# Two norms of a fused two-block model, taken token piece by token piece across the stage boundary

## The chip, the cores and the metric

The kernel runs on one core of one Trainium2 chip. The metric is device time in microseconds (us) from launch to the last result, median of three runs. All arithmetic is in fp32; most matrix products are split in three products of two reduced-precision parts (below).

## The reference, cut to what matters

Two blocks run one after the other on 1024 tokens of width 1024. Block 1 is one hybrid layer; block 2 puts 16 meta tokens in front and runs two layers.

```
# block 1
x = x + mix @ w_out                      # 8 output units of 128 channels
h2 = rmsnorm(x, norm2_g)                 # mean over the 1024 channels, per token
ff = square(relu(h2 @ w_up)); x = x + ff @ w_down      # d_ff 4096
x = rmsnorm(x, final_g)
# block 2, l = 0, 1
h = rmsnorm_2(h_res, norm_gain[l]); proj = h @ w_in[l]
... pooling, latent attention with rotary angles cos/sin(pos * inv_freq) ...
h_res = h_res + merged @ w_out[l]
```

Each norm needs the squares of all 1024 channels of a token before it can scale any of them, and nothing from other tokens.

## The kernel before

**Layout.** Channels lie on the 128 partitions, in 8 chunks (KC = 8), tokens on the free axis: 1024 columns in block 1, 1044 (16 meta, 1024, 4 padding) in block 2. X is the residual, `Ah`/`Al` (act_hi, act_lo) hold an activation as a rounded high part and a low part, `Wh`/`Wl` (w_hi, w_lo) two slots of weights in the same form. R is a work area of 19 rows. The PSUM tile `acc` has two sides s = 0, 1 with three banks each, `aux` has two banks.

**A unit** is 128 output channels of one matrix: 8 chunks k, for each the products Wh·Ah, Wh·Al, Wl·Ah over all columns, in pieces of 512 columns in block 1 (`PIECES1` = 2 x 512) and 348 in block 2 (`PIECES2` = 3 x 348). So a unit is 48 or 72 matmuls on TensorE (PE). Units alternate the side of `acc` and the weight slot.

**Weights.** SyncE loads each unit's raw weights. GpSimd (POOL) splits them: one cast to Wh (L374), then four subtractions of 256 columns for Wl (L353). It may start on unit n once unit n-2 is done, since the slot must be free. `wide` (L425 inside `matrix`) begins with the products of Wh and waits for Wl later; `wide_two` runs two units side by side, chunk by chunk as the activation arrives, and needs both parts of both units at once.

**The end of a stage.** VectorE (DVE) adds each finished unit to X (L1634), ScalarE (ACT) squares it (L944), DVE adds the square to a total (L1426). After the eighth unit `norm_sum` sums the total over partitions with a matmul of ones (L502). ACT turns that into the scale by Ln and Exp (L949, L952). Then `normalise` on DVE goes through the 8 chunks at full width: multiply (L1433), cast to Ah (L1416), subtract to Al (L1417). PE consumes chunk k as soon as its low part is there.

This happens at two places that the change touches. **Boundary A** lies between block 1's output projection and its feed-forward stage; there the first feed-forward unit runs alone with the arriving chunks (`wide(..., (a_ready, 16))`), and the table of rotary angles (fetch of the positions, 14 DVE operations L1648 to L1665, two sines on ACT L1125 and L1128) follows the norm. The relu that clears `acc` for the third unit (L1138) stands behind the sines in ACT's order. **Boundary B** lies between the first and the second layer of block 2; there `wide_two` runs the first two units side by side. At B, ACT also starts a store of all of X to memory (`spill_x`, L1166), and DVE's pooling (from L1713), which overwrites parts of X, waits for it.

The order on each engine is the order in which the code is written; semaphores join the engines.

Of the kernel before, what the change touches and what calls it, by code (L numbers as in the profile page):

```python
# [7 lines left out]
F32 = mybir.dt.float32  # L8
F32R = mybir.dt.float32r
I32 = mybir.dt.int32  # L10
ALU = mybir.AluOpType
# [125 lines left out]
def build(nc, xT, metaT, pos, params, consts, bands, lru_w, wstream, outT):  # L137
    with ExitStack() as ctx:
# [143 lines left out]
        for name in tuple(f"x_in{j}" for j in range(KC)) + tuple(f"reload{j}" for j in range(KC)) + (  # L282
# [15 lines left out]
            "s_ready", "p_in",  # L298
            "pv_done", "pv_ready0", "pv_ready1", "inv_ready", "inv_used", "av_free0", "av_free1",
# [5 lines left out]
        SQL = ((R[:, 6, :], R[:, 3, :], R[:, 2, :]), (R[:, 7, :], R[:, 1, :], R[:, 0, :]))  # L305

# [94 lines left out]
        def _(pe):  # L401
# [92 lines left out]

            def norm_sum(s, pieces, squares):
# [112 lines left out]
            for j in range(2, KC):  # L608
                wide(j % 2, (j + 1) % 2, PIECES1)
            norm_sum(1, PIECES1, R[:, 8, :])  # L610

            with pe.Fori(0, GROUPS) as i:
                loop = Loop(i, GROUPS, [(unit, FG + 4), (unit_hi, FG + 4), (free[0], FG // 2 + 4),
                                        (free[1], FG // 2 + 4), (c["f_ready"], FG)])
                for j in range(FG):
                    wide(j % 2, (j + 1) % 2, PIECES1, (sems["a_ready"], 16) if j == 0 else None)
                for j in range(4):
                    next_unit()
                    ws = (j + 1) % 2
                    for s in range(2):  # L620
                        if j == 0 and s == 0:
# [3 lines left out]
                               None if s == 0 else sems["unit_done"])  # L625
                loop.end()
            norm_sum(0, PIECES1, R[:, 8, :])

            a_count = 24
            ws0 = N_UNITS1 % 2  # L630
            for l in range(LAYERS):
# [6 lines left out]
                norm_sum(0, PIECES2, R[:, 8, :])  # L638
                wide_two(PIECES2, (sems["a_ready"], a_count), (ws(), ws()))
                for j in range(2, 8):  # L640
                    wide(j % 2, ws(), PIECES2)
                a_count += 8
# [254 lines left out]
                for j in range(2, KC):  # L897
                    wide(j % 2, ws(), PIECES2)
                a_count += 8
# [4 lines left out]
        def _(act):  # L904
# [49 lines left out]
            def norm_stats(src, n, width, pieces, s, slots, rs, dim, eps, arrive):  # L954
# [3 lines left out]
                norm_scale(width, pieces, s, rs, dim, n)  # L958

# [151 lines left out]
            def updated(s):  # L1111
# [5 lines left out]
            norm_stats(lambda j: X[:, j, META:T2], KC, T1, PIECES1, 1, SQ, R[:, 10, :],  # L1117
                       DM, 1e-6, lambda j: updated(j % 2))
            act.dma_start(X[:, :, 0:META], metaT.rearrange("(c p) t -> p c t", p=P)).then_inc(sems["meta_in"], 16)
            act.wait_ge(sems["a_ready"], 24)  # L1120
            act.dma_start(R[:, 8, META:T2].bitcast(I32), pos).then_inc(sems["pos_in"], 16)

            c["to_act"].step()
            act.wait_ge(sems["to_act"], c["to_act"].value())
            do(nc.scalar.activation(R[:, 16, 0:TP], R[:, 16, 0:TP], ACT.Sin))  # L1125
# [256 lines left out]
        def _(dve):  # L1382
# [254 lines left out]
            for j in range(KC):  # L1637
                await_unit()
                add_to_residual(j, j % 2, PIECES1, META, T1)
                if j:  # L1640
                    add_square(j - 1, KC, SQ, full)
# [461 lines left out]
```

## Time and profile before

| | us |
|---|---|
| median of 3 runs (3355.52 to 3359.7) | 3358.72 |
| the profiled execution: its own time | 3356.4 |
| its span, first to last instruction | 3354.6 |
| PE busy in the span | 3057.1 (91%) |
| DVE busy | 1440.9 (43%) |
| POOL busy | 1074.3 (32%) |
| ACT busy | 694.5 (21%) |

The profiled execution's own time is its span and 1.8 us around it; it lies 2.3 us below the median. PE is busy for most of the span, so what counts is where PE stands idle and what ended its wait. Matmul records overlap: the distance of two starts is the cost of one.

### The profile page before, as it was taken

The page shows a single profiled execution, that of the slowest core. Times are in us where ns is not written, and L with a number is a line of the kernel's source. Part 1 is how long each engine was busy: PE and PEld are TensorE (multiplying, and loading weights), DVE is VectorE, ACT ScalarE, POOL GpSimd, SP SyncE. Part 2 cuts the span into 40 slices and gives each one's busy share as a digit, 9 for nine tenths or more (in the row PEclk, how much of TensorE's full clock was granted, in tenths as well). Part 3 has the DMA queues.
Part 4 walks back from the last instruction along what each step waited for, and adds up shares of the span by engine and source line. Part 5 has one row for each costly group of instructions (what it writes and reads, how often), then busy time and mean ns, then how long its engine had stood idle before and what let it go on. Part 6 is the DMA issues. An engine that isn't in the chain of part 4 may idle for free.

```text
span 3354.6 us, 41151 instructions
## 1 busy us (share of the span) xinstructions
PE 3057.1 (91%) x16352; PEld 2688.7 (80%) x16352; DVE 1440.9 (43%) x1730; ACT 694.5 (21%) x1239; POOL 1074.3 (32%) x1335
## 2 busy tenths in 40 slices
PE   6976678899999997799999899989899999999999
PEld 4754556677788775699999788889899999788889
DVE  4678454422222223830011666671820111766661
ACT  2132320000000001100111455510100110455500
POOL 3523013344444443333333211133433432211132
PEclk9988789999999998899999999999899999999999
DMA  2101011111111111211212000051211212000042
GB/s 104 44 32 35 1 63 39 49 46 44 50 44 47 47 44 44 77 51 45 102 45 83 32 14 14 14 185 45 89 51 45 96 51 77 32 16 18 15 178 76
DMA packets 46429, 182.50 MB, mean 54 GB/s; under 512 B 5968, under 2 KB 6096, under 8 KB 45776
## 3 DMA queue, kind: packets, MB, share of 16 engines
q1 hardware_dynamic: 31248, 113.19, 10.6%
q10 hardware_dynamic: 15040, 67.28, 5.3%
q8 instruction: 107, 1.75, 0.2%
q14 instruction: 34, 0.28, 0.0%
HBM read 150.06 MB, written 30.39 MB: 54 GB/s over the span
## 4 chain that ended last, share of the span: by engine, by line
PE 80%; DVE 13%; ACT 3%; issue 2%; POOL 1%; DMA 0%; DVEq 0%; ACTq 0%; POOLq 0%; SPq 0%
PE acc L425 59%; PE aux L824 4%; PE acc L708 4%; PE acc L803 3%; DVE act_lo L1417 2%; PE acc L757 2%; PE acc L692 1%; DVE residual L1482 1%; DVE work L1433 1%; DVE work L1426 1%; PE acc L778 1%; DVE act_hi L1416 1%; PE acc L720 1%; POOL w_lo L353 1%; DVE residual L1505 1%
## 5 line engine op out<-in xcount | busy, mean ns | idle before, releaser
L425 PE MATMUL acc<-act_hi,w_hi 128*128 128x348 f32 (+1 forms) x3104 | 770.6, 349 | 100.7 <-DVE act_lo L1417 41.2
L353 POOL TENSOR_TENSOR w_lo<-w_raw,w_hi 128x256 fp32r<-128x256 f32 (+1 forms) x924 | 817.3, 916 | 17.2
L425 PE MATMUL acc<-act_lo,w_hi 128*128 128x348 f32 (+1 forms) x3104 | 763.9, 346 | 0.0
L425 PEld LDWEIGHTS acc<-act_hi,w_hi 128*128 128x128 f32 x3104 | 546.3, 191 | 162.4 <-issue 68.1
L425 PE MATMUL acc<-act_hi,w_lo 128*128 128x348 f32 (+1 forms) x3104 | 618.8, 345 | 0.0
L425 PEld LDWEIGHTS acc<-act_lo,w_hi 128*128 128x128 f32 x3104 | 548.8, 190 | 43.1
L425 PEld LDWEIGHTS acc<-act_hi,w_lo 128*128 128x128 f32 x3104 | 530.0, 189 | 42.1
L373 POOL TENSOR_TENSOR small<-shape_consts 128x1 f32<-128x1 f32 x192 | 40.9, 213 | 1607.0 <-PE acc L425 1607.0
L425 PE MATMUL acc<-ff_split,w_hi 128*128 128x512 f32 (+1 forms) x1408 | 317.7, 375 | 11.9 <-DVE ff_split L1417 11.9
L1634 DVE TENSOR_TENSOR residual<-acc,residual 128x1024 f32<-128x1024 f32 (+1 forms) x88 | 108.1, 1228 | 473.0 <-PE acc L425 472.9
L425 PEld LDWEIGHTS acc<-ff_split,w_hi 128*128 128x128 f32 x1408 | 253.0, 188 | 60.8 <-DVE ff_split L1417 16.5
L362 POOL CAST w_hi<-w_raw 128x1024 fp32r<-128x1024 f32 x23 | 25.8, 1122 | 632.6 <-PE acc L708 544.4
L1846 DVE TENSOR_REDUCE small<-acc 128x1 f32<-128x512 f32 (+4 forms) x240 | 132.1, 550 | 192.5 <-PE acc L761 121.9
L803 PE MATMUL acc<-ff_split 128*128 128x276 f32 (+5 forms) x864 | 208.4, 354 | 0.0
L374 POOL CAST w_hi<-w_raw 128x1024 fp32r<-128x1024 f32 x192 | 202.5, 1055 | 0.0
L824 PE MATMUL aux<-work 128*128 128x276 f32 (+5 forms) x576 | 177.3, 404 | 0.0
L425 PE MATMUL acc<-ff_split,w_lo 128*128 128x512 f32 (+1 forms) x704 | 166.8, 374 | 0.0
L803 PEld LDWEIGHTS acc<-ff_split 128*128 128x128 f32 x864 | 140.8, 190 | 31.3 <-ACT work L1307 0.5
L1138 ACT ACTIVATE work<-acc 128x1024 f32<-128x1024 f32 x32 | 32.7, 1027 | 627.0 <-PE acc L425 626.4
L932 ACT ACTIVATE work<-acc 64x384 f32<-64x384 f32 (+5 forms) x153 | 93.5, 620 | 289.2 <-PE acc L425 255.7
L1307 ACT ACTIVATE work<-acc 128x384 f32<-128x384 f32 (+2 forms) x240 | 104.2, 435 | 233.9 <-PE acc L803 160.6
L425 PEld LDWEIGHTS acc<-ff_split,w_lo 128*128 128x128 f32 x704 | 127.2, 188 | 22.5
(228 smaller groups left out, 3307.6 us busy)
## 6 DMA issues: line engine op xcount, KB each, us to landing
w_raw<-in_wstream SPq DMA_DIRECT2D x215, 512.0 KB, 3.5
spill_x<-residual ACTq DMA_DIRECT2D x2, 4176.0 KB, 12.2
spill_m<-residual ACTq DMA_DIRECT2D x2, 4176.0 KB, 12.6
spill_g<-work ACTq DMA_DIRECT2D x16, 522.0 KB, 2.7
residual<-spill_m ACTq DMA_DIRECT2D x16, 522.0 KB, 6.1
work<-spill_g ACTq DMA_DIRECT2D x16, 522.0 KB, 8.6
residual<-spill_x ACTq DMA_DIRECT2D x16, 522.0 KB, 4.3
residual<-in_xT ACTq DMA_DIRECT2D x8, 512.0 KB, 9.9
```

Source lines behind the costliest of these rows:

```text
L353: ins = nc.gpsimd.tensor_tensor(Wl[:, s, c0:c0 + w], Wraw[:, s, c0:c0 + w], Wh[:, s, c0:c0 + w].bitcast(F32), ALU.subtract)
L374: nc.gpsimd.tensor_copy(Wh[:, s, :], Wraw[:, s, :]).then_inc(sems["w_hi_done"], 1)
L425: ins = nc.tensor.matmul(acc[0:m, s, p, 0:w], wt[:, ws, w0 + j * m:w0 + j * m + m], x[:, k, p * w:p * w + w], start=(first and t == 0), st ...
L708: ins = nc.tensor.matmul(acc_q[:, 0:w], wt[:, w_head[0], j * P:j * P + P], x[:, j, c0:c0 + w], start=(j == 0 and t == 0), stop=(j == 5 and ...
L757: ins = nc.tensor.matmul(acc_r[bank][:, 0:n], qh[:, min(P * i, LASTQ):min(P * i, LASTQ) + P], kh[:, 512 * p:512 * p + n], start=True, stop ...
L803: ins = nc.tensor.matmul(out, k2[kt][:, c0:c0 + P], q2[qt][:, lo:lo + w], start=m == 0, stop=(m == 2 and not diag))
L824: ins = nc.tensor.matmul(aux[:, b % 2, lo - QP * pc:lo - QP * pc + w], values(h)[:, t, :], prob(k)[:, at:at + w], start=t == 0, stop=end)
L932: return nc.scalar.activation(out, in_, ACT.Copy, scale=scale)
L1307: do(nc.scalar.activation(prob(k)[:, 0:w], src, ACT.Exp), "p_in")
L1417: do(vec.tensor_tensor(lo, src, hi.bitcast(F32), ALU.subtract), name)
L1634: do(vec.tensor_tensor(x, acc_view(s, pieces), x, ALU.add), f"free{s}")
L1846: do(vec.tensor_reduce(S_[:, col:col + 1], acc_r[rough_bank(i, p)][:, 0:n], AX, ALU.max, negate=True), "rough_max")
```

## The change

The last two output units of a stage now run piece by piece: piece 0 of both, then piece 1 of both, and so on (`close_two`). DVE adds a finished piece to X, ACT squares it, and a small matmul into `aux` (`sum_piece`) sums it while PE is in the next piece. DVE and ACT then normalise this piece (`norm_pieces`), ACT making the high part. The first two units of the next stage also run piece by piece (`open_two`); in its first piece the first unit goes four chunks ahead of the second. The order of the steps is the table `NORM_ORDER`. The same is done at A (2 x 512) and at B (3 x 348). The rotary table is computed during the output units before A. `spill_x` at B is issued after the last piece is normalised. The first of the eight feed-forward groups stands outside the loop.

```diff
+        NORM_ORDER = {
+            2: (("add", 0), ("norm", 0, 0, 4), ("add", 1), ("norm", 0, 4, 6), ("norm", 0, 6, 8), ("norm", 1, 0, 8)),
...
+        NORM_SCALE_AFTER = {2: (0, 3), 3: (0, 3, 6)}
+            def sum_piece(p, w):
+                c["piece_total"].step()
+                pe.wait_ge(sems["piece_total"], c["piece_total"].value())
...
+                nc.tensor.matmul(aux[:, p % 2, 0:w], ones, R[:, 8, p * w:p * w + w], start=True,
+                                 stop=True).then_inc(sems["piece_summed"], 1)
+            def close_two(ws, pieces):
+                n, w = pieces
+                for p in range(n):
+                    for s in range(2):
+                        if p == 0:
+                            next_unit()
+                            await_low()
+                            take(s)
+                        for k in range(KC):
+                            ins = piece_products(s, ws[s], p, w, k, k == 0, k == KC - 1)
...
+                            if p and s == 0 and k == 4:
+                                sum_piece(p - 1, w)
+            def open_two(ws, pieces):
...
+                for p in range(n):
+                    ahead = 4 if p == 0 else 0
+                    at = 0
+                    for j in range(KC + ahead):
+                        for s, k in ((0, j), (1, j - ahead)):
...
+                            if k == 0:
+                                if p == 0:
+                                    next_unit()
+                                    await_low()
...
+                            if s == 0:
+                                pe.wait_ge(sems["piece_lo"], lo0 + KC * p + k + 1)
+                            ins = piece_products(s, ws[s], p, w, k, k == 0, k == KC - 1)
...
+                            if p == 0 and at == 8:
+                                sum_piece(n - 1, w)
@@ tensor, boundary A
-            for j in range(2, KC):
+            for j in range(2, KC - 2):
                 wide(j % 2, (j + 1) % 2, PIECES1)
-            norm_sum(1, PIECES1, R[:, 8, :])
...
+            close_two((1, 0), PIECES1)
+            open_two((1, 0), PIECES1)
@@ scalar
+            def norm_pieces(x0, pieces):
...
+                for at, step in enumerate(NORM_ORDER[n]):
...
+                    if step[0] == "add":
...
+                            do(nc.scalar.activation(sq[s][:, cols], X[:, KC - 2 + s, x0 + p * w:x0 + p * w + w],
+                                                    ACT.Square), "piece_squared")
+                    else:
+                        for j in range(step[2], step[3]):
...
+                            do(copy(Ah[:, j, cols], y[j % 2][:, cols]), "piece_hi")
+                    if at in NORM_SCALE_AFTER[n]:
...
+                        act.wait_ge(sems["piece_summed"], c["piece_summed"].value())
+                        do(nc.scalar.activation(R[:, 10, cols], aux[:, p % 2, 0:w], ACT.Ln, scale=1.0 / DM,
+                                                bias=eps_col(1e-6, P)))
+                        after()
+                        do(nc.scalar.activation(R[:, 10, cols], R[:, 10, cols], ACT.Exp, scale=-0.5), "piece_scale")
...
+            act.dma_start(R[:, 13, META:T2].bitcast(I32), pos).then_inc(sems["pos_in"], 16)
+            for j in range(KC - 2):
+                updated(j % 2)
+                square(X[:, j, META:T2], j, [t[:, 0:T1] for t in SQ])
+                if j == 4:
...
+                    do(nc.scalar.activation(R[:, 16, 0:TP], R[:, 16, 0:TP], ACT.Sin))
@@ vector
+            def norm_pieces(x0, pieces, gain):
...
+                            do(vec.tensor_tensor(x, acc[:, s, p, 0:w], x, ALU.add),
+                               "piece_free" if p < n - 1 else f"free{s}")
...
+                    def low(j):
...
+                        do(vec.tensor_tensor(Al[:, j, cols], y[j % 2][:, cols], Ah[:, j, cols].bitcast(F32),
+                                             ALU.subtract), "piece_lo")
...
+                        do(vec.scalar_tensor_tensor(y[j % 2][:, cols], X[:, j, x0 + p * w:x0 + p * w + w],
+                                                    param(gain, j), R[:, 10, cols], ALU.mult, ALU.mult), "piece_y")
+                        if j > step[2]:
+                            low(j - 1)
```

On DVE at boundary A this stood after the totals (STT multiplies, CAST makes the high part, the last row subtracts; one chunk of eight is shown, then the start of the rotary table):

```order
L1433 SCALAR_TENSOR_TENSOR work<-residual,params,work 128x1024
L1416 CAST act_hi<-work 128x1024
L1417 TENSOR_TENSOR act_lo<-work,act_hi 128x1024
L1648 TENSOR_SCALAR work<-work 128x1024
L1649 COPY work<-shape_consts 128x16
L1650 MEMSET work 128x4
L1653 TENSOR_SCALAR work<-work,params 128x1044
```

And now, from the residual adds of piece 0 of the last two units (first row) to the same adds of piece 1 and the first chunks behind them:

```order
L1564 TENSOR_TENSOR residual<-acc,residual 128x512 x2
L1569 TENSOR_TENSOR work<-work 128x512 x2
L1583 SCALAR_TENSOR_TENSOR work<-residual,params,work 128x512 x2
L1576 TENSOR_TENSOR act_lo<-work,act_hi 128x512
L1583 SCALAR_TENSOR_TENSOR work<-residual,params,work 128x512
L1576 TENSOR_TENSOR act_lo<-work,act_hi 128x512
L1583 SCALAR_TENSOR_TENSOR work<-residual,params,work 128x512
L1576 TENSOR_TENSOR act_lo<-work,act_hi 128x512 x2
L1564 TENSOR_TENSOR residual<-acc,residual 128x512 x2
L1569 TENSOR_TENSOR work<-work 128x512 x2
L1583 SCALAR_TENSOR_TENSOR work<-residual,params,work 128x512 x2
```

The casts have left DVE, the operations are half as wide, and four chunks of piece 0 stand ahead of the adds of piece 1.

On ACT at boundary A stood the squares of the eight units, then the scale, two transfers and the sines:

```order
L944 ACTIVATE work<-residual 128x1024 x8
L949 ACTIVATE work<-acc,small 128x1024
L952 ACTIVATE work<-work 128x1024
L1119 DMA residual<-in_metaT 128x8x16
L1121 DMA work<-in_pos 128x1024
L1125 ACT_TABLE_LOAD
L1125 ACTIVATE work<-work 128x1044
```

And now (L1064 squares a piece, L1076 and L1079 are Ln and Exp of a piece's sum, L1018 makes high parts):

```order
L1030 ACTIVATE work<-residual 128x1024
L1064 ACTIVATE work<-residual 128x512 x2
L1076 ACTIVATE work<-aux,small 128x512
L1079 ACTIVATE work<-work 128x512
L1018 ACTIVATE act_hi<-work 128x512 x4
L1064 ACTIVATE work<-residual 128x512 x2
L1018 ACTIVATE act_hi<-work 128x512 x2
L1076 ACTIVATE work<-aux,small 128x512
L1079 ACTIVATE work<-work 128x512
L1018 ACTIVATE act_hi<-work 128x512 x10
```

The scale of piece 1 stands between the high parts of chunks 5 and 6 of piece 0; the sines are no longer behind the scale.

## Rows read from the trace of the kernel before

**Rows 1.** The page: chain that ended last, shares of the span.
```profile
PE 80%; DVE 13%; ACT 3%; issue 2%; POOL 1%; DMA 0%; DVEq 0%; ACTq 0%; POOLq 0%; SPq 0%
```

**Rows 2.** Timeline, PE, boundary A: start, us, engine, line, operation [idle before <-releaser].
```profile
545.56 0.62 PE L425 MATMUL acc<-act_hi,w_hi 128*128 128x512 f32 x2
...
561.79 3.75 PE L502 MATMUL acc<-work,shape_consts 128*128 128x512 f32 x4 [4.95 <-DVE work L1426]
...
571.31 1.19 PE L425 MATMUL acc<-act_hi,w_hi 128*128 128x512 f32 x2 [5.77 <-DVE act_lo L1417]
...
595.87 0.62 PE L425 MATMUL acc<-act_hi,w_hi 128*128 128x512 f32 x2
...
616.14 1.22 PE L425 MATMUL acc<-act_hi,w_hi 128*128 128x512 f32 x2 [8.98 <-ACT work L1138]
...
629.32 0.62 PE L425 MATMUL acc<-act_hi,w_hi 128*128 128x512 f32 x2
...
640.44 1.09 PE L425 MATMUL acc<-ff_split,w_hi 128*128 128x512 f32 x4
```

**Rows 3.** The chain of waits, boundary A: fetch of the positions, first sine.
```profile
594.35 3.44 DMA work<-in_pos
...
612.22 1.08 ACT work L1125
```

**Rows 4.** Timeline, PE, boundary B.
```profile
2328.17 0.64 PE L425 MATMUL acc<-act_hi,w_hi 128*128 128x348 f32 x3
...
2339.62 0.64 PE L425 MATMUL acc<-act_hi,w_hi 128*128 128x348 f32 x3
...
2392.40 0.74 PE L425 MATMUL acc<-act_hi,w_hi 128*128 128x348 f32 x3
...
2403.96 0.64 PE L425 MATMUL acc<-act_hi,w_hi 128*128 128x348 f32 x3
```

**Rows 5.** Groups by line and form, DVE and ACT: xcount | busy us, mean ns | idle before.
```profile
L1822 DVE SCALAR_TENSOR_TENSOR residual<-residual,params 128x384 f32<-128x384 f32 x32 | 19.8, 619 | 1.1
L1599 DVE TENSOR_TENSOR residual<-shape_consts,small 128x512 f32<-128x512 f32 x12 | 8.3, 693 | 0.4
L1826 DVE TENSOR_TENSOR ff_split<-residual,ff_split 128x276 fp32r<-128x276 f32 x16 | 7.1, 447 | 0.6
L1278 ACT ACTIVATE residual<-residual 128x384 f32<-128x384 f32 x32 | 16.8, 524 | 1.0
```

**Rows 6.** Timeline, POOL: the split of one unit's weights, DVE idle, DVE partly and wholly busy.
```profile
489.76 2.83 POOL L353 TENSOR_TENSOR w_lo<-w_raw,w_hi 128x256 fp32r<-128x256 f32 x4
...
2341.18 3.90 POOL L353 TENSOR_TENSOR w_lo<-w_raw,w_hi 128x256 fp32r<-128x256 f32 x4
...
2398.86 6.74 POOL L353 TENSOR_TENSOR w_lo<-w_raw,w_hi 128x256 fp32r<-128x256 f32 x4
```

**Rows 7.** Timeline, DVE, beside the last of these splits, and the end of the pooling.
```profile
2392.24 1.26 DVE L1713 TENSOR_TENSOR residual<-work 128x1059 f32<-128x1059 f32 x1 [2.77 <-ACT work L932]
...
2401.63 1.68 DVE L1713 TENSOR_TENSOR residual<-residual 128x1057 f32<-128x1057 f32 x1
...
2429.96 1.25 DVE L1728 TENSOR_TENSOR work<-acc,work 128x1044 f32<-128x1044 f32 x1
```

**Rows 8.** Timeline, PE: the start behind a wait for weights that POOL had to split.
```profile
1839.44 1.21 PE L425 MATMUL acc<-act_hi,w_hi 128*128 128x348 f32 x3 [4.34 <-POOL w_lo L353]
...
1842.18 0.76 PE L425 MATMUL acc<-act_hi,w_hi 128*128 128x348 f32 x3
```

**Rows 9.** Busy us by engine, then granted clock, DMA share, GB/s, in that stretch.
```profile
1839.00:1842.00 3.00, 2.56 (x9) 2.59 (x10) 0.00 (x0) 0.00 (x0) 0.19 (x1) 0.50 0.48 154
```

**Rows 10.** Timeline, PE: matmuls of 384 columns, each with other operands than the last.
```profile
1998.45 0.34 PE L708 MATMUL acc<-act_lo,w_hi 128*128 128x384 f32 x1
1998.63 0.34 PE L708 MATMUL acc<-act_hi,w_lo 128*128 128x384 f32 x1
```

**Rows 11.** The page: DMA issues, us to landing.
```profile
spill_x<-residual ACTq DMA_DIRECT2D x2, 4176.0 KB, 12.2
```

More of the change, by code:

```diff
@@ new lines, in piece_products @@
+            def piece_products(s, ws, p, w, k, first, end):
+                for t, (wt, x) in enumerate(((Wh, Ah), (Wh, Al), (Wl, Ah))):
+                    ins = nc.tensor.matmul(acc[:, s, p, 0:w], wt[:, ws, k * P:k * P + P],
+                                           x[:, k, p * w:p * w + w], start=(first and t == 0), stop=(end and t == 2))
+                return ins
+            def close_two(ws, pieces):
[8 more added lines that the diff above has]
+                            ins = piece_products(s, ws[s], p, w, k, k == 0, k == KC - 1)
+                            if k == KC - 1:
+                                ins.then_inc(sems["piece_done" if p < n - 1 else "unit_done"], 1)
+                            if p and s == 0 and k == 4:
+                                sum_piece(p - 1, w)
@@ L607, in _, with expand_group @@
             wide_two(PIECES1, (sems["a_ready"], 8), (1, 0))
-            for j in range(2, KC):
+            for j in range(2, KC - 2):
                 wide(j % 2, (j + 1) % 2, PIECES1)
-            norm_sum(1, PIECES1, R[:, 8, :])
[L612 to L616, printed above, removed]
+            close_two((1, 0), PIECES1)
+            open_two((1, 0), PIECES1)
+            def expand_group(first):
+                for j in range(2 if first else 0, FG):
+                    wide(j % 2, (j + 1) % 2, PIECES1)
                 for j in range(4):
@@ L896, in _ @@
                 wide_two(PIECES2, (sems["a_ready"], a_count), (ws(), ws()))
-                for j in range(2, KC):
+                for j in range(2, KC - 2):
                     wide(j % 2, ws(), PIECES2)
+                if l == LAYERS - 1:
+                    for j in range(KC - 2, KC):
+                        wide(j % 2, ws(), PIECES2)
+                else:
+                    close_two((ws(), ws()), PIECES2)
                 a_count += 8
@@ L1421, in add_square @@
+            def add_square(j, n, slots, cols, last="sum_ready"):
                 c["sq_ready"].step()
@@ L1940, in _ @@
                     split(y, Ah[:, j, :], Al[:, j, :], "a_ready")
-                for j in range(KC):
+                for j in range(KC if last else KC - 2):
                     await_unit()
@@ L1945, in _ @@
                     if not last and j:
-                        add_square(j - 1, KC, SQ, wide)
+                        add_square(j - 1, KC - 2, SQ, wide)
                 if not last:
-                    add_square(KC - 1, KC, SQ, wide)
+                    add_square(KC - 3, KC - 2, SQ, wide, "dve_step")
+                    for j in range(KC - 2, KC):
+                        dve.wait_ge(sems[f"reload{j}"], 48 * (l + 1))
 def weight_stream(w):
```

185 lines of the change are left out of this document (136 added, 49 removed).

## The prediction, written before the changed kernel was run

> **What bounds the kernel now.** I read the chain that ended last first: PE holds 80% of it, DVE 13% [rows 1]. So most of the time is matmul time, which this change leaves as it is; it can only win where the chain leaves PE. The timeline of PE at the two boundaries shows how much that is. All times below are counted from a zero at the start of the seventh output unit.
>
> Boundary A. The eighth output unit starts at 545.56, a unit lasts 640.44 - 629.32 = 11.12 us, so the zero is 534.44. The third feed-forward unit starts at 616.14 and ends at 629.32, which is zero + 94.9 [rows 2]. In that stretch PE has five units of work, 55.6 us, and a short sum. The rest of about 39 us is: the wait of 4.95 for the totals; 9.5 us until the first product (the sum at low clock and 5.77 of waiting for ACT and DVE); the first feed-forward unit alone, 571.31 to 595.87, 24.6 us for 11.1 us of work, since DVE delivers a chunk only every 3.1 us; 9.0 us before the third unit, which waits for the relu that stands on ACT behind the sines; and 13.18 us instead of 11.12 for that third unit, which starts at low clock [rows 2]. The chain there goes through the fetch of the positions, the 14 operations of the angle table and the sines [rows 3].
>
> Boundary B. Unit length 2339.62 - 2328.17 = 11.45, zero 2328.17, third unit of the next layer from 2392.40 to 2403.96, which is zero + 75.8 [rows 4]. Five units are 57.3 us, so 18.5 us are lost; it is less than at A because two units already run side by side and no angle table follows.
>
> **The change, part by part.** Prices first. A matmul of 512 columns costs 11.12/48 = 0.232 us, one of 348 columns 11.45/72 = 0.159 us [rows 2, 4]. So a chunk of one unit in one piece (three matmuls) is 0.695 at A and 0.477 at B. For DVE's narrow operations I take the nearest widths: 0.62 for the multiply at 384 columns, 0.69 at 512, 0.45 for a subtraction at 276 [rows 5]; with 0.03 of issue between, that makes multiply and subtraction together 1.50 us per chunk at 512 and 1.16 at 348. Before, a chunk took 24.6/8 = 3.1 at full width, so two pieces (3.0) are no dearer than one whole, because the cast is ACT's now. ACT's high part is 0.52 at 384 [rows 5], about 0.63 at 512; it runs beside DVE's next multiply and is seen only at the end of each run of chunks, some 0.7 us.
>
> *Weights are the new term.* `close_two` and `open_two` need both parts of both units. POOL may split a unit only when the one two before it is done; that costs it some 1.3 us of cast and start, then 2.83 for the four subtractions with DVE idle, 3.90 with DVE partly busy, 6.74 with DVE wholly busy [rows 6]. In that last stretch DVE's operation takes 1.68 in place of 1.26 [rows 7]: the two alternate, one slice of POOL (1.68) for each DVE operation, and DVE loses 0.42. With DVE operations of 0.5 to 0.7 us the same alternation gives about 1.0 us a slice, so a split is 5.5 to 6.5 us and takes 2 to 3 us of DVE time.
> The Trainium skill ("SBUF — State Buffer", section "Who interferes with whom") says that a DVE instruction with two SBUF inputs and a GpSimd instruction that reads SBUF exclude each other, the first holding the port for its whole length. The alternation agrees; the size does not: a slice alone is 0.71, and DVE loses 0.42 for it, not 0.71. By the rule's size the eight slices at A would cost DVE 2.3 us more, and the time would be about 2 us above my sum; the sum goes by the rows.
>
> *Boundary A, after, from the zero.* Piece 0 of both units ends at 11.1 (+0.5 for the eighth unit's weights, ready 5.5 after its start as before). Adds, squares and totals of half width: piece total at about 14. PE reaches the sum after five chunks, 14.9, and spends 0.9 (the two sums of the old form took 3.75 at half the clock [rows 2]). Ln and Exp: scale at 17.3. Piece 1 ends at 23.8, PE having worked without a gap. DVE has from 17.3 four chunks of piece 0 (6.0 + 0.7), stretched by 2 us since POOL now splits the first two feed-forward units; then the four adds and totals of piece 1 (2.9, stretched to 3.5), then chunks 4 and 5. So chunks 0 to 3 are there at the end of piece 1, and chunk 4 only at about 31.5. PE works 4 x 0.695 and waits 4.7 us for chunk 4. It restarts at low clock, at a price of 1.3 to 2.1: after a wait of 4.34 three groups of three matmuls took 2.74 us in place of 1.43, with a granted clock of 0.50, the lower level of 1.2 GHz [rows 8, 9]; after 8.98 the third unit took 2.06 more [rows 2]. Four more chunks and the sum of piece 1 bring PE to 37.0. Now the order on ACT bites: Ln and Exp of piece 1 stand ahead of the high parts of chunks 6 and 7 of piece 0, which the DVE subtractions and then PE wait for. Chunk 6 is complete at 40.1, so PE waits 3.1 us again. Then 8 chunks to 45.8 and 16 chunks of piece 1 (11.1; DVE, which began piece 1 at about 40.8 and needs 12 us, stays ahead) to 57.0. The third unit waits 0.9 for POOL's cast and takes 11.1: it ends at 69.0, against 94.9. Gain 25.9.
>
> The angle table: fetch and angles move beside output units. The 14 operations took 612.22 - 597.79 = 14.4 us [rows 3]; they are cut in three portions of at most five, so some 6 us each, beside units in which DVE otherwise has two full-width operations of 1.26 [rows 7], 2.5 to 3 of 11.1 us. The two sines and the relu behind them took 3.9 us on ACT (612.22 to 616.14 [rows 2, 3]), which has one operation of that kind per unit. So it costs nothing; without this cover at most 9 us would return, the wait of before. The table loads of ACT have no row here; up to 6 us of them would still fit in a unit.
>
> *Boundary B, after.* Four units 45.8 and three sums 1.8 make 47.6. In piece 0, s = 1 starts after 3.8 us, but its weights are ready 5.5 after the unit's start (2341.18 + 3.90 - 2339.62 [rows 4, 6]): 2.0 us with the restart. The piece chain (8.2 us of PE per piece) just keeps up: 3 chunks, four adds and totals, and 5 chunks are 2.3 + 9.3 + 1.4 us over two pieces. At the start of the next stage PE waits 0.9 for the first unit's weights (their split started one third of a unit early, at the seventh unit's end) and 1.9 for the second's, partly covered by the four chunks ahead. From there DVE is ahead of PE. Sum with restarts 53.1; then 1.1 for POOL's cast and 11.5: the third unit ends at 65.7 against 75.8. Gain 10.1.
> Its price on the other side: the store of X is issued after the last high part, at about 49.4, and takes 12.2 us [rows 11], to 61.6. The pooling on DVE would start at about 55 otherwise and lasts 37.7 us (2392.24 to 2429.96 [rows 7]); it now ends at about 99.5 with its first product, and the seventh unit of the layer needs that side of `acc` at 99.9. So the store costs between 0 and 3 us; I take 0.6.
>
> *Cost nothing*: the first feed-forward group outside the loop, the half-width residual adds (same columns), the new semaphore waits of PE where the value is there already. Bounds: 0 and 0.5 together, by the 0.1 that three matmuls behind a wait take longer than the next three (0.74 and 0.64 [rows 4]).
>
> Sum: 25.9 + 10.1 - 0.6 = 35.4, less 0.9 for the chance that the wait of 3.1 at A also lowers the clock: 34.5. Profiled execution 3356.4 - 34.5 = 3321.9; the median of the runs stands 2.3 above it, so **3324**.
>
> **Rivals.**
> 1. *Narrow operations don't collide with POOL.* Speaks for it: in the stage of the heads 276-wide subtractions take 0.45 and show no stretch of 0.42 [rows 5]; against it, POOL was mostly idle there, and the collision is plain where both are busy [rows 6, 7]. Then the splits take 4.1 us, DVE loses nothing, chunk 4 is there 3 us earlier and the clock stays up: gains 30.5 and 12.3, time about 3316.
> 2. *The in-order waits feed on each other.* If each of the waits of 2 to 5 us lowers the clock (two at A, two at B, 1.3 to 2.1 each) and the store holds back the pooling by 3 us, the gain is about 25 and the time 3334; with handovers between three engines at 0.1 to 0.2 for each of 40 chunk pieces on the path, up to 3340.
> 3. *Slower: the weight loads come into the open.* Piece by piece, each of the 480 matmuls of the four times two paired units has another stationary operand than the one before it or shares it with one only; before, it was kept for two or three in a row. If a load then stood in front of each, at the length of a matmul of 384 columns (0.18 [rows 10]), that would be 480 x 0.18 = 86 us, less 35, time about 3410; it decides from 35/480 = 0.073 us per matmul on. Against it: rows of 384 columns with high, low and weight-low products in turn start 0.18 us apart, no more per column than here, so the loads were hidden [rows 10].
> 4. *No change*: what PE gains at the boundary is lost in the stage behind. Against it, the feed-forward groups and the layer's units are PE's own pace with waits of 1 us.
>
> **How the numbers follow.** Forecast case 0.62 (3318 to 3331), rival 1 0.14 (3311 to 3318), rival 2 0.20 (3331 to 3343), rival 3 0.02, rival 4 0.02. The range of 8 in 10 takes the forecast case, most of rival 1 and the nearer part of rival 2: 3313 to 3338. 0.2% is 6.7 us, about what this measurement can tell from no change. Faster by more: 0.96; within: 0.02; slower: 0.02.
>
> **What would show it.** At A PE's timeline should hold a wait of 4 to 5 us for a DVE subtraction after the fourth chunk of the new stage, a second one of about 3 us for the seventh, and the third feed-forward unit ending 69 us after the start of the seventh output unit (65 by rival 1, over 72 by rival 2); no 9 us before that unit. At B waits for POOL of about 2, 1 and 2 us, and the third unit's end at 66. POOL's splits beside `norm_pieces` should last 5.5 to 6.5 us, narrow DVE operations beside them be 0.4 longer than alone. Matmul distances must remain 0.232 and 0.159. I am wrong if either boundary gains less than half of its sum, or if the first product of the pooled branch holds PE for more than 3 us.

## The result, and the profile after

| | before | after |
|---|---|---|
| median of the runs, us | 3357.1 (3354.9 to 3359.7, 4 runs) | 3327.2 (3327.0 to 3328.7, 4 runs) |
| ratio | | 0.9912, 95% interval 0.9894 to 0.9929 |
| profiled execution, span, us | 3356.4, 3354.6 | 3327.1, 3325.3 |
| PE, DVE shares of the chain | 80%, 13% [rows 1] | 82%, 11% |
| boundary A: zero to third feed-forward unit's end | 94.9 [rows 2] | 72.3 |
| boundary B: zero to third unit's end | 75.8 [rows 4] | 70.1 |

The forecast was 3324, the time is 3327.2: faster, inside the range, 3 us longer than forecast. The two boundaries gave 22.6 and 5.7 us where the sum had 25.9 and 10.1. Together that is 28.2 of the 29.3 us between the spans. The other 1.1 is 2.0 gained behind boundary B, where the code is the same, less 0.9 lost ahead of A and between the two; the last experiment shows the stretch behind B to scatter by more than that.

Boundary A, PE's timeline after: start, us, engine, line, operation, in brackets the idle time before it and what ended it. It answers to [rows 2].

```profile
534.76 0.40 PE L516 MATMUL acc<-act_hi,w_hi 128*128 128x512 f32 x1
...
559.87 0.47 PE L516 MATMUL acc<-act_hi,w_hi 128*128 128x512 f32 x1 [0.98 <-issue]
...
567.90 0.79 PE L516 MATMUL acc<-act_hi,w_hi 128*128 128x512 f32 x1 [5.00 <-DVE act_lo L1576]
568.49 0.63 PE L516 MATMUL acc<-act_lo,w_hi 128*128 128x512 f32 x1
...
573.10 1.02 PE L510 MATMUL aux<-work,shape_consts 128*128 128x512 f32 x2
576.88 0.80 PE L516 MATMUL acc<-act_hi,w_hi 128*128 128x512 f32 x1 [2.75 <-DVE act_lo L1576]
...
595.84 0.74 PE L434 MATMUL acc<-act_hi,w_hi 128*128 128x512 f32 x2 [0.68 <-POOL w_hi L383]
...
607.09 0.62 PE L434 MATMUL acc<-act_hi,w_hi 128*128 128x512 f32 x2
```

The waits of 4.95, 5.77 and 8.98 are gone, and so is the slow pace of the first unit. Two new ones stand in their place, for `act_lo`: 5.00 behind the fourth chunk of the new stage and 2.75 for the seventh. The 9 us before the third unit are 0.68. Before 559.87 PE works through the last two output units with one wait of 0.67.

ACT in that stretch shows where the second wait is from.

```profile
567.15 0.63 ACT L1018 ACTIVATE act_hi<-work 128x512 fp32r<-128x512 f32 x1 [0.16 <-DVE work L1583]
574.16 0.69 ACT L1076 ACTIVATE work<-aux,small 128x512 f32<-128x512 f32 x1 [6.38 <-PE aux L510]
574.88 0.63 ACT L1079 ACTIVATE work<-work 128x512 f32<-128x512 f32 x1
575.41 1.13 ACT L1018 ACTIVATE act_hi<-work 128x512 fp32r<-128x512 f32 x2
```

ACT stands 6.38 us for PE's sum of piece 1 (573.10), with the high parts of chunks 6 and 7 behind it (575.41). PE itself came to that sum late, out of its wait for chunk 4.

Boundary B after, PE's timeline, against [rows 4].

```profile
2306.56 0.32 PE L516 MATMUL acc<-act_hi,w_hi 128*128 128x348 f32 x1
...
2312.96 0.40 PE L516 MATMUL acc<-act_hi,w_hi 128*128 128x348 f32 x1 [2.42 <-issue]
...
2336.54 0.40 PE L516 MATMUL acc<-act_hi,w_hi 128*128 128x348 f32 x1 [1.56 <-issue]
...
2341.65 0.63 PE L516 MATMUL acc<-act_hi,w_hi 128*128 128x348 f32 x1 [2.48 <-issue]
...
2365.12 0.74 PE L434 MATMUL acc<-act_hi,w_hi 128*128 128x348 f32 x3 [0.90 <-POOL w_hi L383]
...
2376.68 0.64 PE L434 MATMUL acc<-act_hi,w_hi 128*128 128x348 f32 x3
```

The three waits put down to "issue" are for low parts of weights. POOL's splits end just before each wait does:

```profile
2308.05 4.81 POOL L362 TENSOR_TENSOR w_lo<-w_raw,w_hi 128x256 fp32r<-128x256 f32 x4
...
2332.65 3.79 POOL L362 TENSOR_TENSOR w_lo<-w_raw,w_hi 128x256 fp32r<-128x256 f32 x4
...
2337.93 3.62 POOL L362 TENSOR_TENSOR w_lo<-w_raw,w_hi 128x256 fp32r<-128x256 f32 x4
```

What the clock took. Windows of the kernel after: stretch, its length, then PE, PEld, DVE, ACT, POOL busy, granted clock, DMA share, GB/s. All four stand behind the waits of 5.00, 2.75, 2.42 and 2.48.

```profile
568.00:573.00 5.00, 5.00 (x12) 3.94 (x13) 2.08 (x3) 0.00 (x0) 0.00 (x0) 0.50 0.00 2
577.00:579.90 2.90, 2.90 (x7) 2.32 (x8) 2.76 (x5) 1.26 (x2) 0.00 (x0) 0.51 0.00 0
2313.90:2317.00 3.10, 3.10 (x12) 3.10 (x11) 0.00 (x0) 0.00 (x0) 0.00 (x0) 0.50 0.53 169
2341.70:2344.40 2.70, 2.70 (x9) 2.70 (x10) 2.48 (x6) 0.99 (x2) 0.00 (x0) 0.50 0.58 177
```

In all four stretches PE works without a gap and at the lower level of 1.2 GHz. Against distances of 0.232 and 0.159 (they are the same as before, away from the restarts) the slow products cost 5.20 - 12 x 0.232 = 2.4, 3.06 - 7 x 0.232 = 1.4, 3.19 - 11 x 0.159 = 1.4 and 2.75 - 9 x 0.159 = 1.3 us.

### The profile page after: what moved, and what is told of

Its sections match the earlier page's. It is cut to its first block, busy times and chain, and to the rows that moved or that the text cites. A ratio compares the mean times of both kernels' runs of the same rounds, so it can differ in the third digit from the quotient of the medians.

```text
span 3325.3 us, 41282 instructions
## 1 busy us (share of the span) xinstructions
PE 3053.6 (92%) x16352; PEld 2689.1 (81%) x16352; DVE 1448.7 (44%) x1774; ACT 719.5 (22%) x1292; POOL 1072.6 (32%) x1335
## 4 chain that ended last, share of the span: by engine, by line
PE 82%; DVE 11%; ACT 3%; issue 2%; POOL 1%; DMA 0%; DVEq 0%; POOLq 0%; ACTq 0%; SPq 0%
PE acc L434 58%; PE aux L905 4%; PE acc L789 4%; PE acc L884 3%; PE acc L516 3%; PE acc L838 2%; PE acc L773 1%; DVE residual L1652 1%; DVE act_lo L1545 1%; PE acc L859 1%; POOL w_lo L362 1%; PE acc L801 1%; DVE work L1596 1%; DVE work L1603 1%; DVE act_hi L1544 1%
## 5 line engine op out<-in xcount | busy, mean ns | idle before, releaser
L434 PE MATMUL acc<-act_hi,w_hi 128*128 128x348 f32 (+1 forms) x2944 | 726.5, 347 | 70.6 <-ACT residual L1106 19.8
L434 PE MATMUL acc<-act_lo,w_hi 128*128 128x348 f32 (+1 forms) x2944 | 721.3, 345 | 0.0
L434 PEld LDWEIGHTS acc<-act_hi,w_hi 128*128 128x128 f32 x2944 | 517.2, 190 | 123.9 <-issue 53.9
L434 PE MATMUL acc<-act_hi,w_lo 128*128 128x348 f32 (+1 forms) x2944 | 575.2, 345 | 0.0
L434 PEld LDWEIGHTS acc<-act_lo,w_hi 128*128 128x128 f32 x2944 | 518.8, 190 | 39.9
L434 PEld LDWEIGHTS acc<-act_hi,w_lo 128*128 128x128 f32 x2944 | 501.1, 189 | 39.5
L434 PE MATMUL acc<-ff_split,w_hi 128*128 128x512 f32 (+1 forms) x1408 | 317.7, 375 | 11.4 <-DVE ff_split L1545 11.4
L1018 ACT ACTIVATE work<-acc 64x384 f32<-64x384 f32 (+5 forms) x153 | 93.4, 619 | 264.2 <-PE acc L434 227.2
L1852 DVE TENSOR_TENSOR work<-work 128x1024 f32<-128x1024 f32 x32 | 40.9, 1277 | 240.7 <-ACT work L1261 240.6
## 6 DMA issues: line engine op xcount, KB each, us to landing
residual<-in_xT ACTq DMA_DIRECT2D x8, 512.0 KB, 10.1
```

Of the source, the lines that this page charges most:

```text
L434: ins = nc.tensor.matmul(acc[0:m, s, p, 0:w], wt[:, ws, w0 + j * m:w0 + j * m + m], x[:, k, p * w:p * w + w], start=(first and t == 0), st ...
L1018: return nc.scalar.activation(out, in_, ACT.Copy, scale=scale)
```

## Experiments

They are compared by a stretch of PE's timeline, since the median scatters more than most edits are worth: from the start of the seventh output unit to the start of the third unit of the next stage, in us, in the one profiled execution of each kernel. The medians come from four rounds (those of e1 to e11 on three different chips), and each round has its own runs of the kernel before: 3357.1 for after, 3355.2 for e1 to e4, 3354.6 for e5 to e8, 3356.7 for e9 to e11. So medians of different rounds are best compared by the gain on the kernel before of the same round.

| kernel | A | B | median (runs) | gain, same round | ratio to before, 95% |
|---|---|---|---|---|---|
| before | 81.7 | 64.2 | 3357.1 (4) | | |
| after | 61.1 | 58.6 | 3327.2 (4) | 29.9 | 0.9894 to 0.9929 |
| e1, A only | 61.1 | as before | 3332.9 (5) | 22.3 | 0.9919 to 0.9946 |
| e2, table only | 72.6 | as before | 3345.0 (6) | 10.2 | 0.9958 to 0.9982 |
| e3, sum early | 55.9 | 57.3 | 3322.2 (4) | 33.0 | 0.9886 to 0.9916 |
| e4, block order | 53.3 | 57.1 | 3317.7 (4) | 37.6 | 0.9874 to 0.9904 |
| e5, close high first | 60.8 | 54.8 | 3325.1 (4) | 29.4 | 0.9895 to 0.9926 |
| e6, open high first at B | 62.3 | 56.5 | 3326.4 (5) | 28.2 | 0.9900 to 0.9927 |
| e7, all | 51.2 | 52.5 | 3310.8 (4) | 43.8 | 0.9856 to 0.9886 |
| e8, less of POOL | 56.9 | 57.1 | 3318.8 (4) | 35.7 | 0.9877 to 0.9907 |
| e9, after again | 61.1 | 57.3 | 3328.3 (5) | 28.4 | 0.9903 to 0.9930 |
| e10, all, chunk waits | 51.2 | 51.5 | 3309.6 (4) | 47.1 | 0.9846 to 0.9876 |
| e11, e10 with less of POOL | 49.1 | 51.5 | 3309.5 (4) | 47.2 | 0.9842 to 0.9872 |

**e1 and e2: the change in three parts.** e1 gives boundary B its old norm back, e2 both boundaries. Of each edit only PE's part is shown.

```
...
-                if l == 0:
-                    norm_sum(0, PIECES2, R[:, 8, :])
-                    wide_two(PIECES2, (sems["a_ready"], a_count), (ws(), ws()))
-                    a_count += 8
-                else:
-                    open_two((ws(), ws()), PIECES2)
+                norm_sum(0, PIECES2, R[:, 8, :])
+                wide_two(PIECES2, (sems["a_ready"], a_count), (ws(), ws()))
+                a_count += 8
```

e2 does in addition, with the table left where the change put it:

```
...
-            for j in range(2, KC - 2):
+            for j in range(2, KC):
                 wide(j % 2, (j + 1) % 2, PIECES1)
-            close_two((1, 0), PIECES1)
-            open_two((1, 0), PIECES1)
+            norm_sum(1, PIECES1, R[:, 8, :])
```

> Boundary B as before the change (whole-width norm, sum of squares on its own), table and boundary A as after. Theory: the two boundaries add up, and B is worth what its own timeline shows, third unit of the next layer at zero + 70.1 in place of 75.8, 5.7 us: 3327.2 + 5.7 = 3333. Rival (boundary B gave more behind the boundary than at it, since 1.8 us of the gain lie after the pooled branch): 3335 or more. Rival (B gave nothing, waits only moved): 3327.

> Only the rotary table and the fetch of the positions are moved under the output units; both norms run whole as before. Theory: the wait of 9.0 us before the third feed-forward unit goes, with the 2.06 us that this unit lost at low clock, and nothing comes in its place: 3357.1 - 11 = 3346; the piece by piece part of boundary A is then worth 22.5 - 11 = 11.5. Rival: the 14 DVE operations, two sines and table loads delay the output units' adds and squares and PE waits for them there: gain under 6 us, 3351 or more.

Measured: 3332.9 and 3345.0, with 3355.2 for the kernel before beside them. So the pieces at A are worth 12.1 us (in the timeline 11.4) and the table 10.2 (11.2, the restart of the third unit among it). For B the timeline gives 5.7. The medians of e1 and after differ by 5.7 too, but they are from two rounds; by the gains of each round B is worth 6.1 (against e9) to 7.6 (against after). In e2 the old waits of the norm stand as they were, and the third unit starts on time and at full clock.

```profile
559.75 1.19 PE L574 MATMUL acc<-work,shape_consts 128*128 128x512 f32 x1 [4.95 <-DVE work L1582]
...
592.35 0.72 PE L434 MATMUL acc<-act_hi,w_hi 128*128 128x512 f32 x2 [1.64 <-DVE act_lo L1531]
...
604.97 0.62 PE L434 MATMUL acc<-act_hi,w_hi 128*128 128x512 f32 x2
```

The third line has no wait, and the unit lasts 11.1 instead of 13.2: the sines and the 14 operations cost nothing under the output units.

**e3 and e4: the order of PE's work at A.**

In open_two e3 has one edit, and e4 another order of steps (and the sum at 6), of which the new steps are shown:

```
-                            if p == 0 and at == 8:
+                            if p == 0 and at == (4 if n == 2 else 8):
```

```
+                    if p == 0 and n == 2:
+                        steps = [[(0, k) for k in range(4)] + [(1, k) for k in range(4)]]
+                        steps += [((0, k), (1, k)) for k in range(4, KC)]
```

> One number: at boundary A PE takes the sum of the last piece behind four products of the next stage, not eight. Theory: the second wait (2.76 us for a DVE subtraction) is made by the order on PE: the total is ready at 565.6, PE comes to the sum only at 573.1, behind its wait for chunk 4, and ACT's high parts of chunks 6 and 7 stand behind the Ln and Exp of that sum. With the sum first, wait and second low clock go: 7.1 us for eight products become 5.6 and 3.8 of sum and wait go, 5.3 us: 3322. Rival 1 (DVE's rate of chunks is the bound, and chunk 6 comes no earlier): 3327. Rival 2 (wait goes, but the low clock of the first wait stays on longer): 3324.

> Boundary A: PE does chunks 0 to 3 for the first feed-forward unit, then 0 to 3 for the second, then chunks 4 to 7 for both, and the sum of the last piece behind six products. Theory: the 5.0 us wait for chunk 4 comes from the order of products; PE has four products (2.8 us) to do meanwhile, and waits only 2.1 us for the second unit's weights, at 565.0. Piece 0 ends at 573.8 in place of 584.0, DVE then gives a chunk of piece 1 each 1.5 us, and the end of both units comes 9.4 us earlier: 3318. Rival 1 (a wait of 2.1 is enough for the low clock): 3320. Rival 2 (DVE and its collisions set the pace, as the original sum had it): 3325 or more.

e3 took 5.2 us off A (5.3 expected): the wait for chunk 6 and its low clock are gone. PE still stands 2.70 us for the total of piece 1 and 0.67 for chunk 4, at zero + 33.2 as before, and the low clock of that restart stays (twelve slow products). Its ACT has Ln, Exp and the high parts in one run.

```profile
564.80 0.63 ACT L1018 ACTIVATE act_hi<-work 128x512 fp32r<-128x512 f32 x1 [0.16 <-DVE work L1583]
565.34 0.67 ACT L1076 ACTIVATE work<-aux,small 128x512 f32<-128x512 f32 x1
566.04 0.63 ACT L1079 ACTIVATE work<-work 128x512 f32<-128x512 f32 x1
567.05 0.63 ACT L1018 ACTIVATE act_hi<-work 128x512 fp32r<-128x512 f32 x1 [0.38 <-DVE work L1583]
```

e4 took 7.8 us (9.4 expected). Its one wait, for the second unit's low part, brought the low clock after all:

```profile
563.76 0.47 PE L516 MATMUL acc<-act_hi,w_hi 128*128 128x512 f32 x1 [2.17 <-issue]
...
564.76 0.62 PE L516 MATMUL acc<-act_lo,w_hi 128*128 128x512 f32 x1
```

So at both new waits of boundary A there was work that another order could put there: rival 1 of e3 and rival 2 of e4 are out. That does not make DVE's pace free: e8 below shortens the same wait from DVE's side.

**e5, e6, e7: weights.**

piece_products gets the parts that it does (0 and 1 are the products with the high part of the weights, 2 the one with the low part). e5, in close_two; the loop behind it, not shown, does part 2 where p is 0:

```
                         if p == 0:
                             next_unit()
-                            await_low()
                             take(s)
+                            for k in range(KC):
+                                piece_products(s, ws[s], p, w, k, k == 0, False, (0, 1))
+                            await_low()
```

e6, in open_two at B, for a block of chunks k0 to k1 of unit s (0 to 8 of unit 0, the sum, 0 to 8 of unit 1), and e7 at A too (0 to 4 of both):

```
+                        if s == 0:
+                            pe.wait_ge(sems["piece_lo"], lo0 + KC * p + k1)
+                        if k1 - k0 > 1:
+                            for k in range(k0, k1):
+                                piece_products(s, ws[s], p, w, k, k == 0, False, (0, 1))
+                            if k0 == 0:
+                                await_low()
...
+                            for k in range(k0, k1):
+                                piece_products(s, ws[s], p, w, k, False, k == KC - 1, (2,))
```

> In close_two, piece 0 of each unit is done with the high part of the weights first (16 products), then PE waits for the low part and does the other 8. Theory: at boundary B the wait of 2.42 us for the eighth unit's low part is covered by 2.5 us of high products, the low clock behind it (11 products at a distance of 0.29 in place of 0.16, 1.5 us) does not come, and all that follows (total of piece 0, norm, weights of the next stage) moves ahead by 3.9 us; at A the 0.66 goes: 3327.2 - 4.6 = 3322.6. Rival 1 (at B the DVE chain, not PE's waits, sets the end): only part of it shows, 3325 or more. Rival 2 (low clock comes from the work before, not from the wait): 3325.

> At boundary B alone, open_two takes piece 0 of the first unit whole, high part of the weights first, then the sum of the last piece, then piece 0 of the second unit in the same way. Theory: the waits of 1.56 and 2.48 us for low parts and the low clock behind the second (1.5 us) are covered, and DVE's stall of 1.32 us for Ln and Exp of the last piece goes; what is left is DVE's rate of 1.17 us a chunk for 16 chunks (PE needs 0.95): end of both units 3.7 us earlier, 3323.5. Rival 1 (weights hidden, but DVE was the bound already): 3326 to 3327. Rival 2 (all of 5.5 us shows): 3321.7.

> All together: boundary A in the block order (chunks 0 to 3 of one unit, then of the other, then side by side) with the high part of the weights first and the sum of the last piece behind the second unit's high products; close_two with the high part first; boundary B as in the run before this one. Theory, added up: 9.5 (block order) + 4.6 + 3.7 + 0 to 1.4 for the low clock that the block order still had: 3308 to 3309.5. Rival (the edits share the same slack, since DVE's chain is what is left at both boundaries): 3313 or more.

e5: B 3.8 shorter than in the kernel after (2.5 against e9), the 2.42 and its low clock are gone. At A the 0.67 went and chunk 4 came 0.8 earlier, but the low clock behind the two waits cost 0.6 more than in after, and A shows 0.3. e6: 2.1 off B (0.8 against e9), less than 3.7: the 1.56 and 2.48 went, but my block waited for its last chunk, 1.99 us, and ran at a granted clock of 0.50 from 2334.6 to 2338.0, which cost 1.5. The medians show neither gain: on the kernel before of their own round e5 gained 29.4 and e6 28.2, where the kernel after gained 29.9 and, run again as e9, 28.4. That e5 and e6 help at B rests on one profiled execution each.

```profile
2334.07 0.40 PE L518 MATMUL acc<-act_hi,w_hi 128*128 128x348 f32 x1 [1.99 <-DVE act_lo L1609]
```

e7: 9.9 off A and 6.1 off B; 3310.8, in the timeline 16.0 of the 18 to 19 that the theory added up, and between the theory's time and the rival's. It has e6's fault at B (the same 1.99, with a clock of 0.51 behind it) and the same at A (a wait of 3.14 for chunk 3).

**e8: what POOL takes.** The end of the loop over slices is UW // 4 for the first two feed-forward units, UW for all others. So this kernel leaves out three quarters of the low parts of those two units:

```
-                for c0 in range(0, UW, w):
+                for c0 in range(0, end, w):
```

> The kernel as after, but POOL makes only the first of the four slices of the low part for the first two feed-forward units (that part of the computation is left out). It measures what POOL's work beside the norm costs. Theory: DVE, whose narrow operations lose 0.42 us to each slice beside them (1.11 in place of 0.69), saves 2.5 us before chunk 4, the first unit's wait of 0.98 goes, but PE's waits for chunks 4 and 6 stay: 2.5 to 3 us less, 3324.5. Rival 1 (rival 1 of the prediction: the collision is what makes the wait for chunk 4, clock and all): 3321 or less. Rival 2 (no effect on chunk 4): 3326 to 3327.

Chunk 4 came at zero + 31.2 instead of 33.1 (2.0 earlier), PE's wait was still 4.25, and A became 4.2 shorter: more than the theory's 3, less than rival 1's 6. The other 2.2 us are clock: the slow products behind the first wait cost 0.7 less, and behind the second wait, 2.75 as before, the granted clock stayed at 1.00, which saved 1.5. Whether POOL's slices had a part in that is not shown. The gain of 35.7 is 5.8 to 7.3 more than that of the kernel after; 4.2 of it is A. The rest isn't explained by the edit: of the 8.4 us between the two spans, 1.5 lie ahead of A, 1.2 between A and B and 1.5 at B.

**e9, e10, e11: scatter, the best version, DVE as the bound.** e9 is the kernel after, unchanged.

e10 against e7:

```
-                        if s == 0:
+                        if s == 0 and k1 - k0 == 1:
                             pe.wait_ge(sems["piece_lo"], lo0 + KC * p + k1)
                         if k1 - k0 > 1:
                             for k in range(k0, k1):
+                                if s == 0:
+                                    pe.wait_ge(sems["piece_lo"], lo0 + KC * p + k + 1)
                                 piece_products(s, ws[s], p, w, k, k == 0, False, (0, 1))
```

> The changed kernel again, unchanged, beside the two below: it shows how much of what e5 and e6 gave in their medians is scatter. Theory: against the kernel before 29 to 30 us faster; its two boundary stretches (start of the seventh output unit to the start of the third unit behind) within 1.5 us of 61.1 and 58.6, since the length of the low clock behind the same wait differs from execution to execution. Rival (the boundary stretches repeat to 0.3 us, and the scatter lies in the rest of the program alone): 61.1 and 58.6 again.

> As the run with all edits, but PE waits for each chunk of piece 0 by itself within the blocks, not for the last chunk of the block. Theory: the waits of 3.14 us at A and 1.99 at B were made by the block waiting for its last chunk; they shrink, but DVE works without a pause from the first multiply to the last subtraction at both boundaries (31.0 us at A, 36.9 at B) and sets the end: A stays at 51.2 from zero to the third unit, B goes from 52.5 to 51 to 52. Median 3309 to 3310. Rival (PE's waits, not DVE, set the end): A 48.5, B 50, median 3306.

> The run before this one, with three of POOL's four low slices left out for the first two feed-forward units (that part of the computation is left out). Theory: DVE sets the end at boundary A now, so the time that POOL's slices take from DVE shows in full: six slices of 0.42, and what the two casts of POOL cost is kept: A 2.5 to 3 us shorter than in the run before, 48.5. Rival 1 (PE is the bound by then): under 1 us. Rival 2 (a slice costs DVE its whole length of 0.7 to 1.1): 4.5 us or more.

e9 and e10 are as their theories said in A and B (e9's gain, 28.4, is a little under the 29 to 30 expected); e11 took 2.1 off A, under its 2.5 to 3 and far under rival 2's 4.5. e10, the fastest version that computes everything, is 3309.6: 18 us below the kernel after (17 to 19 by the gains of the rounds). PE's waits in the blocks shrank to 0.56 and 0.84, and A didn't move, since DVE works from the first multiply to the last subtraction. e10, then e11, DVE's first and last row:

```profile
551.29 1.54 DVE L1596 SCALAR_TENSOR_TENSOR work<-residual,params,work 128x512 f32<-128x512 f32 x2 [3.62 <-ACT work L1092]
...
580.88 1.43 DVE L1589 TENSOR_TENSOR act_lo<-work,act_hi 128x512 fp32r<-128x512 f32 x2
```

```profile
551.59 2.30 DVE L1600 SCALAR_TENSOR_TENSOR work<-residual,params,work 128x512 f32<-128x512 f32 x2 [3.62 <-ACT work L1096]
...
579.20 1.43 DVE L1593 TENSOR_TENSOR act_lo<-work,act_hi 128x512 fp32r<-128x512 f32 x2
```

That is 31.0 and 29.0 us of DVE: six slices of POOL less, 2.0 us less, 0.33 each. The medians of e10 and e11 are alike and do not show these 2 us. e11's profiled execution lost 5.6 us in the stretch behind boundary B (third unit to the end of the span: 965.9 against 960.3 in e10), which the edit doesn't touch; the same stretch is 960.2 in after and 963.5 in e9. Where this scatter sits is open.

## Why the prediction was nearly right, point by point

*What bounds it, and the sign.* Right: the gain is where the chain left PE, and both boundaries gained; the table costs nothing under the output units, as worked out (e2). The profiled execution was forecast at 3321.9 and took 3327.1, 5.2 us more. The median missed by only 3.2, and that is luck: the forecast put it 2.3 above the profiled execution, as in the kernel before, and in the kernel after it stands 0.1 above.

*Boundary A, 25.9 forecast, 22.6 measured.* The two waits for DVE were forecast at 4.7 and 3.1 and are 5.00 and 2.75, at the chunks that the text named. Two terms of the sum were too small. Chunk 4 came at zero + 33.1, not 31.5. Of these 1.6 us, 0.7 is DVE's start (first multiply at 18.0, not 17.3); 0.5 are the first four chunks, whose stretch by POOL was 3.1 where I had charged 2, while without it they took 6.1 and not 6.7; 0.4 are the adds, the totals and chunk 4 itself. Of the 3.1, 0.7 are a subtraction beside POOL's cast, which I had not priced. The other term is the clock: the restart behind chunk 4 cost 2.4 where 1.3 to 2.1 stood, and the second wait did bring the low clock, 1.4 us, for which only 0.9 stood, at the end of the sum. The first feed-forward unit's low part was left out too, 0.98 us in front of the first product, but that cost nothing: PE stood for chunk 4 behind it, and DVE set when that came. It is in part luck that 5.00 came near 4.7: chunk 4 came 1.6 late, and PE reached its wait 1.3 late, 0.98 of it by the low part. The third unit ends at 72.3; I had written "over 72 by rival 2".

*Boundary B, 10.1 forecast, 5.7 measured.* The mechanism was right (three waits for POOL, DVE not the bound; e5 and e6 take the waits away by covering them), the sizes were not. 2.0 "with the restart" was 2.42 and 1.4; the split ran beside full-width operations of DVE and took 4.81, where I had taken the 3.90 of [rows 6]. 0.9 was 1.56. 1.9 was 2.48 and 1.3: the second split ended 5.1 us after the first, the four chunks ahead gave PE 2.3 us of work, and the sum had no 1.3 for the clock there (its 0.7 for restarts is about what the three waits took beyond their idle time, 0.2 us each). Together 1.8 + 0.7 + 1.9 = 4.4 us, the whole gap. The gain of 5.7 is not far above half of the 10.1, the mark below which I had called myself wrong.

*The collision of DVE and POOL.* The narrow operations stretch by what the prediction said. DVE's rows (beside the cast, beside a slice, alone), then POOL's:

```profile
554.34 1.41 DVE L1576 TENSOR_TENSOR act_lo<-work,act_hi 128x512 fp32r<-128x512 f32 x1
...
556.92 1.11 DVE L1576 TENSOR_TENSOR act_lo<-work,act_hi 128x512 fp32r<-128x512 f32 x1
...
579.16 0.69 DVE L1576 TENSOR_TENSOR act_lo<-work,act_hi 128x512 fp32r<-128x512 f32 x1
```

```profile
553.62 1.58 POOL L383 CAST w_hi<-w_raw 128x1024 fp32r<-128x1024 f32 x1
555.28 4.48 POOL L362 TENSOR_TENSOR w_lo<-w_raw,w_hi 128x256 fp32r<-128x256 f32 x4
...
561.42 3.57 POOL L362 TENSOR_TENSOR w_lo<-w_raw,w_hi 128x256 fp32r<-128x256 f32 x4
```

With POOL beside it the subtraction takes 0.42 more, and a slice of POOL 1.0 us (eight in 8.1) for 1.0 forecast. The forecast's 5.5 to 6.5 for a split has the cast and the start in it, as rival 1's 4.1 has (1.3 and 2.83). Counted in that way the two splits beside `norm_pieces` took 6.3 (553.5 to 559.8) and 5.3 (559.7 to 565.0), near the forecast; their four slices alone took 4.48 and 3.57. Rival 1 is out by these rows. The Trainium skill ("SBUF — State Buffer", section "Who interferes with whom") lets one side block for the other's whole instruction. A slice alone is 0.71; over the stretch DVE lost 0.33 per slice (e10, e11): here it is not the whole length.

*The store of X, 0.6.* It cost nothing here. The pooling waits 11 us for it, but it ends in time:

```profile
2372.03 1.26 DVE L1896 TENSOR_TENSOR residual<-work 128x1059 f32<-128x1059 f32 x1 [10.98 <-DMA spill_x<-residual]
...
2407.55 1.25 DVE L1911 TENSOR_TENSOR work<-acc,work 128x1044 f32<-128x1044 f32 x1
```

The seventh unit of the layer, which needs that side of `acc`, starts at 2411.04, 2.2 us after the last of these. This margin is used up where B gets shorter: in e10 the same unit has to wait for the pooling, 0.47 us (in e11 0.76), so there the store does cost something.

```profile
2393.85 0.40 PE L434 MATMUL acc<-act_hi,w_hi 128*128 128x348 f32 x1 [0.47 <-DVE work L1924]
```

*Rivals.* Rival 2 was half right. All four waits over 2 us lowered the clock, 6.5 us in all, as it said; the store held nothing back, and the sums above close without a term for handovers. That puts the truth between the forecast and its 3334. Rival 3 is out by the distances of the products (0.232 and 0.159 as before), rival 4 by the result.

## What to carry to other kernels

Where two units are worked side by side on data that arrives in pieces, write down for each wait of the in-order engine what it could do instead: here the same products in another order, and the high part of the weights ahead of the low part, were worth 18 us, over half as much as the change itself. Put a small operation that another engine waits for (a sum) ahead of a wait, not behind it. Count a restart behind each longer wait as a term of its own; at B the waits of 1.99 us and more mostly had one, those of 1.56 to 1.58 none. When an engine's operations are stretched, multiply the stretch by the number of partners that really run beside it, casts included.

## What the runs showed of the hardware that I had not expected

The length of a wait did not tell whether the clock falls. The same wait of 2.48 us at B was followed by a granted clock of 0.50 in the kernel after, and of 1.00 in e9, the same program:

```profile
2341.40:2344.00 2.60, 2.60 (x15) 2.39 (x16) 2.39 (x6) 1.39 (x3) 0.00 (x0) 1.00 0.58 189
```

In e7 a wait of 3.14 kept the full clock, where 2.17 in e4 did not:

```profile
558.70:561.50 2.80, 2.80 (x12) 2.31 (x13) 2.69 (x4) 1.27 (x2) 2.80 (x4) 1.00 0.22 89
```

The same wait of 2.75 us at A cost 1.4 us of low clock in after and e9, nothing in e8, and 2.8 in e6, where this part of A runs the unchanged code: 14 slow products instead of 7, and A at 62.3. So a restart behind such waits cost between 0 and 2.8 us here; it is not a fixed price. One profile of a boundary is good to about 1.3 us (B: 58.6 and 57.3; A: 61.1 and 62.3), and differences of that size between two kernels of the table prove nothing by themselves. The Trainium skill ("TensorE: Matmul & The Clock Gate", section "Part 1: The HAM clock gate (the "warmup" mystery)") says that the number of slow products differs between runs of one kernel; the rows of after and e9 agree.
